# Gating routed rows as they leave the bank, storing x2 into the first table, and summing only tables in the tail

## The reference, cut to what matters

```python
x = x + gt_m * y                                   # this x is called x2 below
h = rmsnorm(x, g_ffn) * (1 + sc_f) + sh_f          # h2
# moe(h): six of 64 experts for each token
hid    = silu(xblk @ w1[e]) * (xblk @ w3[e])
routed = sum over the six of  w[token, e] * (hid @ w2[e])
shared = (silu(t @ ws1) * (t @ ws3)) @ ws2
x = x + gt_f * (routed + shared)
y = rmsnorm(x, g_final)
```

## Time and profile before

| what | us |
|---|---|
| runs, median (lowest to highest) | 1508.19 (1505.58 to 1511.75) |
| the profiled execution, its own time | 1507.41 |
| its span | 1505.6 |
| TensorE matmul busy | 1357.6 (90%) |
| VectorE busy | 823.9 (55%) |
| GpSimd busy | 438.8 (29%) |
| ScalarE busy | 207.0 (14%) |

### The profile page before, as it was taken

One profiled execution on the slowest core, in us unless ns is written; L12 is line 12 of the kernel. 1 busy time (PEld: TensorE's weight loads), 2 busy tenths in 40 slices (PEclk: granted clock), 3 DMA queues, 4 the chain that ended last, 5 costly groups with the idle time before them and its releaser, 6 DMA issues.

```text
span 1505.6 us, 17406 instructions
## 1 busy us (share of the span) xinstructions
PE 1357.6 (90%) x5860; PEld 616.6 (41%) x5860; DVE 823.9 (55%) x2088; ACT 207.0 (14%) x347; POOL 438.8 (29%) x379
## 2 busy tenths in 40 slices
PE   4889999999989999899699989989989999879947
PEld 2344454545545554455343433433333333323313
DVE  1048686988988899987233333332433343332327
ACT  1121223223131313232000000000000000000003
POOL 0000120212111112224334434444444444453410
PEclk9899999999999999999899999999999999999978
DMA  9988212121121001812999999999999999999976
GB/s 322 334 316 306 107 56 87 42 101 59 70 90 40 33 28 51 251 38 74 357 383 379 366 372 341 392 379 334 377 365 374 372 374 365 346 377 353 371 206 262
DMA packets 96810, 370.74 MB, mean 246 GB/s; under 512 B 18493, under 2 KB 32801, under 8 KB 71967
## 3 DMA queue, kind: packets, MB, share of 16 engines
q1 hardware_dynamic: 73463, 310.40, 53.4%
q0 software_dynamic: 20944, 50.89, 13.1%
q10 hardware_dynamic: 2320, 8.42, 1.4%
HBM read 326.03 MB, written 64.30 MB: 259 GB/s over the span
## 4 chain that ended last, share of the span: by engine, by line
PE 31%; DMA 12%; issue 5%; DVE 2%; POOL 1%; SPq 0%; ACT 0%; POOLq 0%; ACTq 0%
PE U L1017 19%; PE R L1033 9%; DMA acc_rows<-W,kT 5%; DMA acc_rows<-xr,kT 5%; PE X L776 2%; DMA W<-h_rows,q_r 1%; PE T L1023 1%; DMA front<-h_rows,q_r 1%; DVE W L1920 1%; DVE W L1938 1%; DVE W L1935 1%; PE R L1126 0%; DMA W<-acc_rows 0%; POOL W L2005 0%; POOL front L2005 0%
## 5 line engine op out<-in xcount | busy, mean ns | idle before, releaser
L729 PE MATMUL U<-W,front 128*128 128x512 f32 x768 | 343.7, 602 | 1.2 <-issue 1.2
L1435 DVE SCALAR_TENSOR_TENSOR cv<-win,cw,cv 128x128 f32<-128x128 f32 x960 | 256.6, 346 | 1.4
L1017 PE MATMUL U<-W,cat 128*32 128x512 f32 (+2 forms) x848 | 211.9, 625 | 24.4 <-issue 15.9
L1017 PE MATMUL U<-W,front 128*32 128x512 f32 (+2 forms) x1056 | 202.7, 611 | 17.4 <-issue 17.4
L729 PEld LDWEIGHTS U<-W,front 128*128 128x128 f32 x768 | 145.0, 194 | 168.6 <-issue 168.6
L1033 PE MATMUL R<-W,glu 128*32 128x512 f32 (+2 forms) x952 | 207.9, 596 | 1.3 <-DVE glu L1757 1.3
L1744 DVE STREAM_TRANSPOSE front<-front 128x1024 f32<-128x1024 f32 x28 | 57.3, 2045 | 147.9 <-DMA front<-h_rows,q_r 147.9
L1017 PEld LDWEIGHTS U<-W,cat 128*32 128x32 f32 (+2 forms) x848 | 78.2, 147 | 137.2 <-issue 136.1
L2005 POOL DMA_INDIRECT W<-h_rows,q_r x116 | 117.2, 1010 | 48.6 <-issue 34.8
L1033 PEld LDWEIGHTS R<-W,glu 128*32 128x32 f32 (+2 forms) x952 | 71.2, 134 | 131.5 <-issue 130.0
L1744 DVE STREAM_TRANSPOSE cat<-W 128x1024 f32<-128x1024 f32 x29 | 59.2, 2041 | 118.8 <-DMA W<-h_rows,q_r 107.6
(11 more groups left out here) (371 smaller groups left out, 1216.5 us busy)
## 6 DMA issues: line engine op xcount, KB each, us to landing
W<-in_w SPq DMA_DIRECT2D x192, 1024.0 KB, 18.4
W<-in_w_ada SPq DMA_DIRECT2D x24, 1024.0 KB, 8.6
W<-in_w_in SPq DMA_DIRECT2D x6, 2048.0 KB, 19.9
W<-acc_rows SPq DMA_DIRECT2D x16, 512.0 KB, 9.7
front<-in_x_prompt SPq DMA_DIRECT2D x8, 512.0 KB
W<-in_w_out SPq DMA_DIRECT2D x1, 4096.0 KB, 17.8
xr<-in_x_prompt SPq DMA_DIRECT2D x8, 512.0 KB, 4.2
x_rows<-xr SPq DMA_DIRECT2D x8, 512.0 KB, 3.3
```

Of the source, the lines that this page charges most:

```text
L729: last = mm(U[BANK[g]][:, :], hT[:, k, :], w_in[:, k, 512 * g:512 * g + 512], start=k == 0, stop=k == KT - 1)
L1017: last = mm(U[1][cols, :], xgT[z][:, k, cols], w13[:, :, k, :], start=k == 0, stop=k == KT - 1)
L1435: ins = v.scalar_tensor_tensor(cv[:, c, :], win[:, c, w:w + P], cw[:, c, w:w + 1], cv[:, c, :], ALU.mult, ALU.add)
```

## The change

1. x2 tiles are stored into the first table itself, so its prompt rows need no clearing, and no x2 rows are read back. Six clears of 1 MB are left of ten. The sample x2 rows go to a small array of their own.
2. The rows of each block are gated as they leave PSUM: `blk_y` multiplies by the routing weight and by a tile `gate_t`, which a new VectorE instruction `gate(x)` writes for each block: `gt_f` for prompt rows, 1 for rows of sample tokens. Two small instructions at the start make the two columns that choose.
3. The shared rows are gated in one instruction (`sh_out`) and stored by the ScalarE queue: the first three tiles (`EARLY = 3`) straight into the second table, ahead of the line, the others into `shared_rows`. The first three down products run before block 0; the other six run at blocks 8, 14, ..., 38. Nothing is loaded on the ScalarE queue any more.
4. GpSimd waits for all x2 stores before its first scatter, and for the three early shared stores before block 3, the first with a row of the second table. Experts are given tables by their place in their group.
5. In the tail VectorE adds the two tables (and the shared tile for tiles 3 to 7); the sums on TensorE, the gating and the x2 add are gone.

```diff
+EARLY = 3
+SHARED_AT = (-1,) * EARLY + tuple(8 + 6 * n for n in range(NT - EARLY))
-                sp.dma_start(x2_rows[bass.ds(m * P, P), :], xr[:, :]).then_inc(x2_stored, 16)
+                sp.dma_start(acc_rows[bass.ds(m * P, P), :], xr[:, :]).then_inc(x2_stored, 16)
+            sp.dma_start(acc_rows[SEQ:TABLE, :], t["zeros"]).then_inc(spare_in, 16)
             with sp.Fori(2, TP - 1) as i:
-                sp.dma_start(acc_rows[bass.ds(i * 2 * P - 4 * P, 2 * P), :], t["zeros"]).then_inc(spare_in, 16)
...
-            for i in range(TP):
-                sp.dma_start(x2_t[i], x2_rows[P * i:P * i + P, :]).then_inc(x2_in, 16)
+            for i in range(EARLY, TP):
+                sp.dma_start(shared_t[i - EARLY], shared_rows[P * i:P * i + P, :]).then_inc(x2_in, 16)
...
             sh_up_part(2, 1, 0, 0, 4)
+            sh_down(0)
             spread_lists()
             sh_up_part(2, 1, 0, 4, KT)
             sh_up_part(2, 1, 1)
+            sh_down(1)
+            sh_down(2)
...
-            for i in range(1, TP):
-                pe.wait_ge(acc_in[i], acc_there[i])
-                pe.wait_ge(gated, floor(i - 1))
-                for half in (slice(0, 512), slice(512, 1024)):
-                    for x in (acc_t[i], odd_t[i]):
-                        last = mm((X, R)[i % 2][:, half], ident[:, :], x[:, half], start=x is acc_t[i], stop=x is odd_t[i])
...
-            def sh_add(n):
+            def sh_out(n):
                 dve.wait_ge(sh_downs, n + 1)
+                if n > 1:
+                    dve.wait_ge(sh_stored[n % 2], 16 * (n // 2))
...
+                    v.tensor_tensor(sh_y[n % 2], X[:, :], gt_f, ALU.mult).then_inc(sh_copied, 1)
...
+            def gate(x):
+                if x > 0:
+                    dve.wait_ge(y_evac, x)
+                v.tensor_scalar(gate_t, gt_f, gate_on[:, x:x + 1], gate_off[:, x:x + 1], ALU.mult, ALU.add).then_inc(gate_ready, 1)
...
-                v.tensor_scalar(y_sbs[x % 2], R[:, :], slot_w[:, x:x + 1], None, ALU.mult).then_inc(y_evac, 1)
+                v.scalar_tensor_tensor(y_sbs[x % 2], R[:, :], slot_w[:, x:x + 1], gate_t, ALU.mult, ALU.mult).then_inc(y_evac, 1)
...
                 blk_hidT(x)
                 if x in SHARED_AT:
-                    sh_add(SHARED_AT.index(x))
+                    sh_out(SHARED_AT.index(x))
+                gate(x)
                 if x + 2 < NX:
                     xpose(x + 2)
...
             sh_hid_part(2, 0)
+            dve.wait_ge(x2_in, 16)
+            sh_out(0)
             dve.wait_ge(slot_posed, 1)
...
+            v.tensor_scalar(gate_on, U[0][:, 256:256 + NU], float(SEQ), None, ALU.is_lt)
+            v.tensor_scalar(gate_off, U[0][:, 256:256 + NU], float(SEQ), None, ALU.is_ge)
             v.tensor_tensor(slot_i[:, 0:NU], U[0][:, 256:256 + NU], slot_base, ALU.add).then_inc(slot_ready, 1)
             dve.wait_ge(slot_ready, 1)
+            sh_hid_part(2, 1)
+            sh_out(1)
             xpose(0)
-            sh_hid_part(2, 1)
+            sh_out(2)
...
             for i in range(TP):
-                if i == 0:
-                    dve.wait_ge(acc_in[i], acc_there[i])
-                    link(v.tensor_tensor(acc_t[i], acc_t[i], odd_t[i], ALU.add))
-                    ins = v.tensor_tensor(acc_t[i], acc_t[i], gt_f, ALU.mult)
-                else:
-                    dve.wait_ge(sum_done, i)
-                    ins = v.tensor_tensor(acc_t[i], (X, R)[i % 2][:, :], gt_f, ALU.mult)
-                ins.then_inc(gated, 1)
-                dve.wait_ge(gated, i + 1)
-                v.tensor_tensor(acc_t[i], acc_t[i], x2_t[i], ALU.add).then_inc(x3_ready, 1)
+                dve.wait_ge(acc_in[i], acc_there[i])
+                ins = v.tensor_tensor(acc_t[i], acc_t[i], odd_t[i], ALU.add)
+                if i >= EARLY:
+                    link(ins)
+                    ins = v.tensor_tensor(acc_t[i], acc_t[i], shared_t[i - EARLY], ALU.add)
+                ins.then_inc(x3_ready, 1)
                 if i > 0:
                     finish(i - 1)
...
-            pool.wait_ge(spare_in, 16 * 10)
+            pool.wait_ge(spare_in, 16 * 6)
+            pool.wait_ge(x2_stored, 16 * TP)
             for x in range(NX):
                 if x + 3 < NX:
                     gather(x + 3)
+                if x == ODD_FIRST:
+                    for n in range(2):
+                        pool.wait_ge(sh_stored[n], 16 * ((EARLY + 1 - n) // 2))
                 scatter(x)
```

More of the change, by code:

```diff
@@ L81 @@
 NU = len(QUARTERS) // 4
+TABLE_OF = tuple(i % 2 for group in GROUPS for i in range(len(group)))
+ODD_FIRST = min(n // 4 for n, (x, _) in enumerate(QUARTERS) if TABLE_OF[x])
 assert NU % 2 == 1 and all(len({x for x, _ in QUARTERS[4 * u:4 * u + 4]}) < 3 for u in range(NU))
@@ L101 @@
 GROUP = 3
-SHARED_AT = tuple(8 + 4 * n for n in range(NT))
+EARLY = 3
+SHARED_AT = (-1,) * EARLY + tuple(8 + 6 * n for n in range(NT - EARLY))
 F32, BF16, I32 = mybir.dt.float32, mybir.dt.bfloat16, mybir.dt.int32
@@ L235, in build @@
         xg_b, y_sb_b = (W[:, (RING + 1) * WE + D * i:(RING + 1) * WE + D * i + D] for i in range(2))
-        x2_t = [shw[:, D * i:D * i + D] for i in range(6)]
+        shared_t = [shw[:, D * i:D * i + D] for i in range(TP - EARLY)]
         acc_t = [W[:, WE + D * i:WE + D * i + D] for i in range(TP)]
@@ L357, in build @@
         slot_w = kT[:, 1, 0:64]
+        gate_on, gate_off = kT[:, 2, 0:NU], kT[:, 3, 0:NU]
+        more_on, more_off = k_d[:, 152:153], k_d[:, 153:154]
         slot_base = k_d[:, 192:192 + NU]
@@ L578, in _ @@
             sp.wait_ge(s_dve, S_X2)
-            for rows, piece in pieces(x2_rows[SEQ:TOKENS, :]):
+            for rows, piece in pieces(x2_rows_s):
                 sp.dma_start(piece, xs[rows, :]).then_inc(s_rows_stored, 16)
@@ L1120, in _ @@
             pe.wait_ge(y_evac, NX)
-            for i in range(1, TP):
-                pe.wait_ge(acc_in[i], acc_there[i])
-                pe.wait_ge(gated, floor(i - 1))
-                for half in (slice(0, 512), slice(512, 1024)):
-                    for x in (acc_t[i], odd_t[i]):
-                        last = mm((X, R)[i % 2][:, half], ident[:, :], x[:, half], start=x is acc_t[i], stop=x is odd_t[i])
[L1127 to L1130, removed]
+            pe.wait_ge(fin_ssq, 1)
+            mm(T0[:, 0:1], same_row, ssq_f[TP], start=True, stop=True).then_inc(rows_summed, 1)
         @block.scalar
@@ L1318, in _ @@
             score(TP - 1)
[L1319 to L1323, removed]
-                load_x2(n)
+            sh_silu_part(1, 0)
+            sh_silu_part(1, 1)
+            sh_silu_part(2, 0)
+            act.wait_ge(spare_in, 16 * 6)
+            store_shared(0)
+            sh_silu_part(2, 1)
+            store_shared(1)
+            store_shared(2)
             def blk_silu(n):
@@ L1335, in _ @@
                     store_shared(SHARED_AT.index(x - 1))
-                if x - 3 in SHARED_AT and SHARED_AT.index(x - 3) + 2 < TP:
-                    n = SHARED_AT.index(x - 3)
-                    act.wait_ge(sh_stored[n % 2], 16 * (n // 2 + 1))
-                    load_x2(n + 2)
             act.wait_ge(rounds_known, 1)
@@ L1883, in _ @@
             xpose(1)
+            gate(0)
             blk_hid(0)
@@ L1890, in _ @@
             xpose(3)
+            gate(1)
             block(2)
@@ L1908, in _ @@
                         v.tensor_copy(slot_cur, more[:, 0:1]).then_inc(more_ready, 1)
+                        v.tensor_scalar(more_on, more[:, 0:1], float(SEQ), None, ALU.is_lt)
+                        v.tensor_scalar(more_off, more[:, 0:1], float(SEQ), None, ALU.is_ge).then_inc(gate_ready, 1)
+                        dve.wait_ge(gate_ready, NX + 2 * b + 1)
+                        dve.wait_ge(y_evac, NX + b)
+                        v.tensor_scalar(gate_t, gt_f, more_on, more_off, ALU.mult, ALU.add).then_inc(gate_ready, 1)
                         dve.wait_ge(gathered[0], 64 * EVEN + 64 * b + 64)
@@ L1913, in _ @@
                         dve.wait_ge(y_done, NX + b + 1)
-                        v.tensor_scalar(y_sbs[0], R[:, :], more[:, 1:2], None, ALU.mult).then_inc(y_evac, 1)
+                        dve.wait_ge(gate_ready, NX + 2 * b + 2)
+                        v.scalar_tensor_tensor(y_sbs[0], R[:, :], more[:, 1:2], gate_t, ALU.mult, ALU.mult).then_inc(y_evac, 1)
             def finish(i):
@@ L2098, in constants @@
         "zeros": np.zeros((2 * P, D)),
-        "slot_base": np.array([[TABLE * (QUARTERS[4 * u + p // 32][0] % 2) for u in range(NU)] for p in range(P)]),
+        "slot_base": np.array([[TABLE * TABLE_OF[QUARTERS[4 * u + p // 32][0]] for u in range(NU)] for p in range(P)]),
         "disp": np.concatenate([every(NE - 1.0 - e), every(np.resize([LINE[x] for x, _ in QUARTERS], 2 * P)), every(LINE), every(CAPS), base], 1),
```

39 lines of the change are left out of this document (17 added, 22 removed).

## The result

The changed kernel takes 1493.9 us (median of four runs, 1491.3 to 1496.2); the kernel before, beside it, 1509.97 us (1505.6 to 1513.7). The ratio is 0.989, with an interval of 0.986 to 0.993. Predicted were 1488.5 us, in a range of 1481 to 1501: the sign and the range hold, and the gain is 16.1 us instead of 19.2. The profiled execution of the changed kernel took 1494.6 us, with a span of 1492.8.

The account below looks back on a forecast made before the run. The prediction held DMA engines and TensorE both full in the line and VectorE the bound of the tail. Terms -10.3, 0, +0.35, 0, -1.0 and -8.3 made -19.2 on 1507.4 us, 1488.2; it predicted 1488.5, range 1481 to 1501.

Parts of the forecast that it names:

- parts 1 and 2: In the line: 4.72 MB less ScalarE-queue traffic (11.8 us) and three fewer shared down products (10.3 us) give -10.3 us.
- part 2: Before block 0: three early shared down products run hidden in waits, 0 us, with ends of -1.0 and +6.
- part 3: Before the first gather: two small unhidden instructions cost +0.35 us, with ends of +0.2 and +0.5.
- part 4: In the line: 57 gates of 1.2 us run in VectorE's idle time ahead of transposes; cost 0, uncovered 68 us.
- part 5: At the last scatter: three fewer shared tiles to load, 3.9 us of DMA time, bring -1.0 us (0 to 2.0).
- part 6: In the tail: the last scaling ends at 1493.9 to 1494.1 instead of 1502.34, -8.3 us, bounds -7 and -9.5.
- as both full resources shrink, I take the smaller: In the line: DMA engines shrink by 11.8 us and TensorE by 10.3, so -10.3 us is charged.
- the first rival: In the line: scatters keep its length, the saved DMA and TensorE time brings nothing; 1499.5 us, chance 0.14.
- the low end: Line, its end and tail: the bound of scatters lifts too, -12, -2, -9.5, -1.0; 1482.9 us, chance 0.03.
- the second rival: At the start of block 0: the cover of the early shared products fails, +6 us; 1494 us, chance 0.06.
- the third rival: In the line: gates and GpSimd issues contend for the SBUF interface; 1585 us, or about 1508; chance 0.05.
- tile 1 at 1467.43, so 2.6 us per tile: In the tail: tile 0 is there at 1464.81, tile 1 at 1467.43, so tiles arrive every 2.6 us.

Follow-up runs that it names:

- both put back: Changed kernel plus nine HBM-to-HBM copies of 0.524 MB on the ScalarE queue and three unread shared down products on TensorE: 1507.85 us, ratio 0.998 to before.
- second pair of profiles: The changed kernel and the kernel before, profiled once more without any edit: 1493.55 us (ratio 0.990), and one run of 1507.05 us for the kernel before.

## Why the prediction was right, and where it was not

| step | predicted | measured |
|---|---|---|
| parts 1 and 2, the line | -10.3 | -9.9 |
| part 2, start of block 0, and its speed | 0 | -0.1 to -0.2, and -1.6 in the line |
| part 3, two small instructions | +0.35 | +0.24 |
| part 4, the gates | 0 | 0 |
| part 5, the end of the line | -1.0 | 0 |
| part 6, the tail | -8.3 | -5.6 to -6.0 |
| sum | -19.2 | -16.9 to -17.5 |

The measured sums are of stretches in the two pairs of profiles, with -11.4 and -11.5 for the line; the medians give -16.1. The 0.8 to 1.4 us between them are less than the spread of the start of the line.

**Parts 1 and 2: right in size by luck, wrong in the reason.** The step "as both full resources shrink, I take the smaller" named TensorE's 10.3 us as the term. With both put back, TensorE's relief alone is worth 2.3 us and the traffic's alone 11.1. The number came out because the term that I had set aside, 11.8 us of traffic, is nearly as large as the one that I took, and at 2.0 instead of 2.5 us per MB it is 9.4. That is luck: had only 2 us of matmuls left, my step would have given 2 us for the line, where the traffic alone is worth 11. A busy share of 0.94 for TensorE beside 1.00 for DMA was not "as full": its six waits for weights were the slack in which 10 us of matmuls fit, and the earlier trace rows showed 33 us of it. Both put back cost the changed kernel 11.4 to 12.1 us, more than the 9.9 of the table, so the copies are not an exact image of what left. Nothing of the gain is left over that the gating or the order of the blocks would have to explain. That the line keeps its length, the first rival, is refuted by its 11.5 us; that the scatters lift too, the low end, didn't come about: the last one still waits for its predecessor.

**Part 2 at the start.** The late start, the second rival, did not come: the products took 3.45 and 3.67 us, the third was 0.8 us too long for its cover, but the transpose of the rows began 10.4 us behind the spread lists instead of 11.4 (10.5 after 10.9 in the second pair of profiles). That block 0 started at 751.25 us and not within 1 us of 746.6, as I had asked, is the shift of all that stands ahead; in the second profile it was 747.0. What I valued too low is the granted clock. It is 0.94 from 733 to 760 us, with TensorE busy for 24.6 us, after 0.87 with 17.4 busy (0.94 to 1.00 in all ten profiles with the change, 0.85 in the second of the kernel before); block 0's 16 matmuls take 6.88 us in the chain instead of 8.67, and the first scatter is issued 21.0 us behind block 0's start instead of 22.6. I had given this an end of -1.0 and taken none of it.

**Part 4.** The row of all 57 gates in the trace of the changed kernel (count, then min/median/max in ns):

```profile
L1757 DVE TENSOR_SCALAR mods<-mods,kT x57: 771/804/1037, 756.4 to 1437.8; 128x1024 f32<-128x1024 f32 x57
```

0.82 us on average, where I took 1.2 between 0.6 and 1.3. The nearest row of the same length, an add of two tensors, takes 1.22 to 1.23 us. By the Trainium skill (VectorE: DVE Perf Modes, mode 2x_2P) this form runs at twice the rate of the other; the trace agrees that it is faster, though its time is shorter by a third and not by a half; no run here shows why. The cover held as forecast. Against the kernel without per-block gates the transposes' idle time falls from 271.7 to 242.9 us and with three to 174.7: 28.8 us for 46.7 us of gates (20.9 in the second profile of the changed kernel, so this sum is rough to 8 us). That the rest of the gates stand in front of no waiting transpose is likely, not shown. Against the kernel before, as I had written the check, it falls by 12.6 only, and by 4.4 in the second pair; VectorE's busy time in the 594 us grew by 25.5 us (210.23 to 235.73), less than the 39.5 us of gates in them, as it lost other work there. So that check was put badly. That the gates lengthen the line, the third rival, is refuted by the kernel with three of them.

**Part 5.** From the end of the last wait for weights to the last scatter the line takes 98.1 us, as before. The last rows leave PSUM at 1442.91 and their scatter is issued 2.06 us later, where it was 2.70: 0.6 us of that wait went, and the blocks ahead gave it back. I had taken the last gap as if all ahead of it stayed in place.

**Part 6 is where 2.3 to 2.7 us went.** The step that failed is "tile 1 at 1467.43, so 2.6 us per tile". Tile 1 came 3.3 us behind tile 0 in the changed kernel, and in the second profile of the kernel before too; the 2.6 us were those of one profile. I read the landing of tile 1 behind tile 0 and carried it on to tile 2, whose semaphore counts tile 3's load as well. In the kernel before, this wait was hidden behind TensorE's slow first sum, which my step had taken away; I asked what is late next and looked at the load's row, not at what its semaphore counts. With the semaphores apart the forecast of 29 us between first add and last scaling comes out at 29.2, with tile 1 still at 3.3 us.

**The rest of the miss** is the base: I built on 1508.2 us for the kernel before, and its median in the four runs beside the changed kernel is 1510.0. That is 1.8 of the 5.4 us between forecast and result. Another 0.5 us is a slip in the sum: the median stood 0.8 us above the profiled execution, and from 1488.2 I went up by 0.3 only. The rest is the tail's 2.3 to 2.7 and the sum's small terms. One reading was off by a slice, too: in the earlier trace rows the DMA engines are at 9 from the twentieth slice on, not from the nineteenth; nothing hung on it.

**What stays open.** Whether the change lengthens the mixer ahead of the line by a microsecond or two, since its clears and stores are not the same there; the spread of 9 us between executions hides it. And why less traffic than the changed kernel's gives so little, and whether the wait for w2 ahead of `up` costs the line anything.

## What to carry to other kernels

Two resources with busy shares of 1.00 and 0.94 are not two bounds: look at whether the second one's waits are for the first, and if they are, charge relief of the first at its time and relief of the second at little (here 0 to 2.3 us of 10). Read beside the shares which queue carries the bytes: a full engine stays full when the line gets shorter, and the bytes of the other queues in the same window tell how far ahead they run. Where a wait is removed, ask of each wait behind it what its semaphore counts; a pair of loads on one semaphore is a hidden tile of latency in the tail, and three on one semaphore make `up` wait for weights that it doesn't read.

## What the runs showed of the hardware that was not expected

- Traffic added to full DMA engines cost 2.0 us per MB for the first 4.72 MB and 2.8 for the next 4.72 MB; 2.46 MB taken away brought about 1 us of line. The rate stayed at 366 to 369 GB/s in all of these kernels.
- A load of 1 MB issued into the full line landed after 18.5 us at the median in the changed kernel. From the issue of the w2 load that ends the last wait for weights to the end of that wait it was 18.0 to 22.7 us, in six profiles of a line that should be the same.
- A float32 scaling with two scalars per partition, 1024 columns from SBUF to SBUF, took VectorE 0.80 us at the median, and up to 1.04 us; the add of two tensors of that size takes 1.22 us. By the Trainium skill (GPSIMD Engine Reference, specifications) VectorE instructions in a 2-port mode or with two SBUF inputs contend with GpSimd for the SBUF interfaces; the runs agree with it for these scalings, with 1.60, 1.64 and 1.74 us for the mean scatter issue beside none, one and three per block. The longest issue was 1.62 us with none, 2.83 with one and 3.13 with three.
- TensorE's granted clock from 733 to 760 us, the stretch around the start of block 0, was 0.94 to 1.00 when the early products ran there and 0.85 to 0.87 without, and the 16 matmuls of block 0 took 6.88 instead of 8.67 us. 0.43 us each is what such a matmul takes in the line, at the upper of the clock's two levels (2.4 GHz); so before, part of block 0 ran below it. Useful work moved into an idle stretch gave 1.6 us beside its own cost of nothing.
